# Output projections that start from their own operands' semaphores instead of a meeting of the engines, behind forgetting attention, HGRN, differential attention and spatial gating

## The reference, cut to what matters

```python
def fox_mixer(h, w_in, b_f, w_out):       # forgetting attention
    ...
    o = o.transpose(1, 0, 3, 2, 4).reshape(B, S, D)
    return o @ w_out
def hgrn2_mixer(h, w_in, lb, onorm_g, w_out):
    ...
    o = o * lax.rsqrt(jnp.mean(o * o, axis=-1, keepdims=True) + RMS_EPS)
    ...
    o = o.reshape(B, S, D).astype(h.dtype) * jax.nn.silu(g)
    return o @ w_out
# second block
    mix = jnp.concatenate([a_out, b_out], axis=-1) @ w_out_even[j]   # diff attention, gated conv
    ...
    mix = spatial_gating(h, w_in_odd[j], sgu_ln_g[j], sgu_ln_b[j], sgu_w[j],
                         sgu_b[j], w_out_odd[j])
```

## Time and profile before

| | |
|---|---|
| median of 3 runs | 3640.46 us (3634.68 to 3640.66) |
| profiled execution | 3639.07 us, its span 3637.3 us |
| PE busy | 3478.2 us (96%) |
| DVE busy | 1954.3 us (54%) |
| ACT busy | 1253.4 us (34%) |
| mean granted TensorE clock | 0.983 of full |

### The profile page before, as it was taken

One profiled execution on the slowest core, in us unless ns is written; L12 is line 12 of the kernel. 1 busy time (PEld: TensorE's weight loads), 2 busy tenths in 40 slices (PEclk: granted clock), 3 DMA queues, 4 the chain that ended last, 5 costly groups with the idle time before them and its releaser, 6 DMA issues.

```text
span 3637.3 us, 56212 instructions
## 1 busy us (share of the span) xinstructions
PE 3478.2 (96%) x23343; PEld 2871.5 (79%) x23343; DVE 1954.3 (54%) x2685; ACT 1253.4 (34%) x1598; POOL 0.2 (0%) x4
## 2 busy tenths in 40 slices
PE   9999999998999999999999989999999887999998
PEld 7778888887788877778887768887887875888887
DVE  4565736436574653565344355344676666845434
ACT  3474424324342441443223343223532113333222
POOL 0000000000000000000000000000000000000000
PEclk9999999999999999999999999999999999999999
DMA  4102232221123222113222212222233002022231
GB/s 155 58 1 93 93 103 93 93 98 42 58 93 104 93 95 98 41 58 104 93 99 98 81 58 93 93 96 101 91 108 137 4 5 91 5 81 93 93 104 70
DMA packets 50432, 297.10 MB, mean 82 GB/s; under 512 B 6848, under 2 KB 7872, under 8 KB 17349
## 3 DMA queue, kind: packets, MB, share of 16 engines
q1 hardware_dynamic: 39376, 269.92, 21.9%
q10 hardware_dynamic: 10868, 24.41, 1.8%
HBM read 283.99 MB, written 10.33 MB: 81 GB/s over the span
## 4 chain that ended last, share of the span: by engine, by line
PE 90%; DVE 7%; ACT 2%; issue 1%; DMA 0%; DVEq 0%; ACTq 0%; PEldq 0%
PE PS L334 13%; PE PS L336 13%; PE PS L335 13%; PE PS L449 8%; PE PS L450 7%; PE PS L451 7%; PE PS L1902 2%; PE PS L1903 2%; PE PS L1904 2%; PE PS L2409 1%; PE PS L1219 1%; PE PS L2826 1%; PE PS L2412 1%; PE PS L1199 1%; PE PS L215 1%
## 5 line engine op out<-in xcount | busy, mean ns | idle before, releaser
L171 DVE TENSOR_TENSOR WL<-W,WH 128x2048 fp32r<-128x2048 f32 x254 | 582.1, 2292 | 729.3 <-ACT WH L161 723.6
L161 ACT ACTIVATE WH<-W 128x2048 fp32r<-128x2048 f32 x254 | 485.8, 1912 | 1105.2 <-PE PS L451 578.0
L334 PE MATMUL PS<-XH,WH 128*128 128x512 f32 x2144 | 837.8, 391 | 4.3 <-issue 4.3
L335 PE MATMUL PS<-XL,WH 128*128 128x512 f32 x2144 | 835.1, 390 | 0.0
L336 PE MATMUL PS<-XH,WL 128*128 128x512 f32 x2144 | 835.0, 389 | 0.0
L334 PEld LDWEIGHTS PS<-XH,WH 128*128 128x128 f32 x2144 | 403.1, 188 | 93.7 <-issue 10.6
L335 PEld LDWEIGHTS PS<-XL,WH 128*128 128x128 f32 x2144 | 403.1, 188 | 84.5 <-issue 1.0
L336 PEld LDWEIGHTS PS<-XH,WL 128*128 128x128 f32 x2144 | 403.0, 188 | 84.0
L689 DVE TENSOR_TENSOR PS<-PS,R 128x512 f32<-128x512 f32 x248 | 170.9, 696 | 442.4 <-PE PS L336 439.8
L449 PE MATMUL PS<-HH,WH 128*128 128x512 f32 (+1 forms) x960 | 374.7, 390 | 1.2
L451 PE MATMUL PS<-HH,WL 128*128 128x512 f32 (+1 forms) x960 | 373.6, 389 | 0.0
(11 more groups left out here) (480 smaller groups left out, 4607.9 us busy)
## 6 DMA issues: line engine op xcount, KB each, us to landing
W<-in_weights SPq DMA_DIRECT2D x254, 1024.0 KB, 4.9
gate_spill<-slots ACTq DMA_DIRECT2D x16, 256.0 KB, 2.1
gates<-gate_spill ACTq DMA_DIRECT2D x2, 2048.0 KB
x_spill<-X ACTq DMA_DIRECT2D x1, 2048.0 KB, 8.0
X<-x_spill ACTq DMA_DIRECT2D x1, 2048.0 KB
out<-X ACTq DMA_DIRECT2D x8, 256.0 KB, 2.1
W<-in_weights SPq DMA_DIRECT2D x2, 512.0 KB, 5.0
X<-in_x ACTq DMA_DIRECT2D x4, 256.0 KB, 7.2
```

Of the source, the lines that this page charges most:

```text
L161: P.e.activation(K.WH[:, s, :], K.W[:, s, :], ACT.Copy).then_inc(P.sem("hi_ready"), P.adds("hi_ready"))
L171: P.e.tensor_tensor(K.WL[:, s, :], K.W[:, s, :], K.WH[:, s, :].bitcast(F32), ALU.subtract).then_inc(P.sem("weights_split"), P.adds("weight ...
L334: P.e.matmul(out, wh[:, k, c], xh[:, k, r], start=(k == 0), stop=False)
L335: P.e.matmul(out, wh[:, k, c], xl[:, k, r], start=False, stop=False)
```

## The change

PE no longer meets ACT and DVE between the four stages and their projections; it ends the stage with `stage_end_open`. ACT and DVE still meet, with PE's contribution, as before. In place of the meeting:

- The subtraction that writes a tile of `XL` now signals `tile_lo`, and PE waits for two of these before each panel (before each of the first two panels in `DiffOut`, where the attention gives four tiles).
- In the first panel, the banks that are still being read come last within each `kk`, and PE waits for their reader's signal just before the first matmul into each.

The same matmuls and the same elementwise work are done.

```diff
-def narrow_pe(K, P, nk, xh, xl, after_wide, late=None):
+def narrow_pe(K, P, nk, xh, xl, after_wide, late=None, tiles=0, held=()):
...
+        if first and held:
+            behind = [bank for bank, _, _ in held]
+            order = [(kk, t) for kk in range(2) for t in [t for t in range(8) if t not in behind] + behind]
+        if k0 < tiles:
+            P.e.wait_ge(P.sem("tile_lo"), P.due("tile_lo", 2))
...
+            for bank, name, k in held:
+                if first and kk == 0 and t == bank:
+                    P.e.wait_ge(P.sem(name), P.due(name, k))
...
 class ForgettingAttention(Stage):
+    tiles_given = 8
+    def banks_held(self):
+        return [(self.OUT[u], "head_taken", 1) for u in range(2)]
...
         def low_part(pair):
             P.e.wait_ge(P.sem("att_out_hi"), P.due("att_out_hi"))
-            P.e.tensor_tensor(K.XL[:, pair, 0:S], K.att_f[:, :], K.XH[:, pair, 0:S].bitcast(F32), ALU.subtract)
+            P.e.tensor_tensor(K.XL[:, pair, 0:S], K.att_f[:, :], K.XH[:, pair, 0:S].bitcast(F32), ALU.subtract).then_inc(P.sem("tile_lo"), P.adds("tile_lo"))
...
-        P.count("head_taken", 2)
...
 class Hgrn(Stage):
+    tiles_given = 8
+    def banks_held(self):
+        return [(1, "o_root", 8)]
...
 class DiffAttention(Stage):
+    tiles_given = 4
+    def banks_held(self):
+        return [(4, "mean_kept", 1), (7, "mean_kept", 1)]
...
-        P.count("mean_kept", 2)
...
 class SpatialGate(Stage):
+    tiles_given = 8
+    def banks_held(self):
+        return [(2, "sgu_biased", 1), (3, "sgu_biased", 1)]
...
+            if isinstance(st, (ForgettingAttention, Hgrn, DiffAttention, SpatialGate)):
+                after.tiles, after.held = st.tiles_given, st.banks_held()
...
-                if onto_wide or st.between_panels or after is not None and after.between_panels or isinstance(after, PostNorm) or isinstance(st, PostNorm) and isinstance(after, (Wide, MixerProjections, Epilogue)) or (isinstance(after, Narrow) and after.after_wide):
+                if onto_wide or st.between_panels or after is not None and after.between_panels or isinstance(after, PostNorm) or isinstance(st, PostNorm) and isinstance(after, (Wide, MixerProjections, Epilogue)) or (isinstance(after, Narrow) and (after.after_wide or after.tiles)):
                     P.stage_end_open()
```

More of the change, by code:

```diff
@@ L466, in body @@
         panel(4 * i + 4, False, False)
+    assert pairs == 1 or not tiles
     P.loop(pairs, body, weights_split=2, tile_done=4)
@@ L752 @@
     then = None
+    tiles, held = 0, ()
     gives_sums = property(lambda self: not self.before_post)
@@ L758, in pe @@
     def pe(self, K, P):
-        narrow_pe(K, P, self.nk, self.xh, self.xl, self.after_wide)
+        narrow_pe(K, P, self.nk, self.xh, self.xl, self.after_wide, None, self.tiles, self.held)
         if not self.before_post:
@@ L1326, in low_part @@
             P.e.wait_ge(P.sem("o_hi"), P.due("o_hi"))
-            P.e.tensor_tensor(K.XL[:, t, 0:S], K.f1[:, t, :], K.XH[:, t, 0:S].bitcast(F32), ALU.subtract)
+            P.e.tensor_tensor(K.XL[:, t, 0:S], K.f1[:, t, :], K.XH[:, t, 0:S].bitcast(F32), ALU.subtract).then_inc(P.sem("tile_lo"), P.adds("tile_lo"))
         for t in range(8):
@@ L1570, in low_part @@
             P.e.wait_ge(P.sem("o_hi"), P.due("o_hi"))
-            e.tensor_tensor(K.XL[:, h, 0:S], K.in2[:, h, :], K.XH[:, h, 0:S].bitcast(F32), ALU.subtract)
+            e.tensor_tensor(K.XL[:, h, 0:S], K.in2[:, h, :], K.XH[:, h, 0:S].bitcast(F32), ALU.subtract).then_inc(P.sem("tile_lo"), P.adds("tile_lo"))
         pad_rows(0)
@@ L1670, in pe @@
         narrow_pe(K, P, self.nk, self.xh, self.xl, self.after_wide,
-                  lambda: P.e.wait_ge(P.sem("conv_lo"), P.due("conv_lo")))
+                  lambda: P.e.wait_ge(P.sem("conv_lo"), P.due("conv_lo")), self.tiles, self.held)
     def act(self, K, P):
@@ L1761, in dve @@
                 P.e.wait_ge(P.sem("sgu_hi"), P.due("sgu_hi"))
-                P.e.tensor_tensor(K.XL[:, t - 2, 0:S], K.v2[:, t - 2, :], K.XH[:, t - 2, 0:S].bitcast(F32), ALU.subtract)
+                P.e.tensor_tensor(K.XL[:, t - 2, 0:S], K.v2[:, t - 2, :], K.XH[:, t - 2, 0:S].bitcast(F32), ALU.subtract).then_inc(P.sem("tile_lo"), P.adds("tile_lo"))
     def act(self, K, P):
```

## The result

The changed kernel takes 3618.32 us, the median of 5 runs (3616.3 to 3620.14), against 3640.46 before: the ratio is 0.9947 with a 95% interval of 0.9936 to 0.9958. The profiled execution took 3619.13 us, with a span of 3617.4, so that 19.9 of the 22.1 us are there to be read. Each later run was timed beside the kernel before on its own chip, and its ratio is to that.

What follows compares the result with a forecast made beforehand. The prediction took TensorE (90% of the chain) as the bound, costing idle time and low clock. Gaps of 14.6 and slow starts of 7.3 us, together 21.9, off 3639.07 gave 3617.2; it said 3618, range 3610 to 3629.

Steps and rivals of the forecast that it cites:

- the forecast's case: At the four projections, gaps and most slow starts go and no other wait comes: 21.9 us gained, chance 0.67.
- The gaps: PE's idle time at the meeting before the four projections, 15.04 us less 0.1 each: 14.6 us gained (13.0 to 15.0).
- The slow start: First panels behind the gaps run at 1.2 GHz; removing this gains 2.6, 1.0, 2.2 and 1.5, together 7.3 us (0 to 8.6).
- All behind the four stages: Everything behind the projections is released by PE's own progress and moves with it; no gain or loss counted.
- Held banks and tile waits: First panels' 17 added waits on tile_lo and banks, counted at nothing; 1.7 us if each cost 0.1.
- The owed splits and the convolution: Second panels' splits have 2.8 to 3.6 us slack, DiffOut's convolution 1.2: nothing counted, up to 2.3 us for the convolution.
- The low clock stays: Rival at the four projections: only the gap goes, the first panels stay at 1.2 GHz; 3624.5 to 3626 us, chance 0.15.
- the rule of the Trainium skill: Transposes don't count as clock activity, so the clock could fall in the stages' ends although PE doesn't stop.
- Moved, not removed: Rival at the second panels: PE waits for the owed splits instead; some 3637 to 3640 us, chance 0.07.
- The slow HGRN: Rival in HGRN: clock at 0.50 instead of 0.86 over 86 us loses 31 us; 3648 us, chance 0.04.

Runs made afterwards that it cites:

- e5: The changed kernel run again, unchanged: 3614.47 us.
- e9: Changed kernel with 5 matmuls that nothing reads ahead of the wait for the states in seven of HGRN's eight heads: 3610.69 us, ratio 0.9926.
- e10: Changed kernel with first-panel bank groups moved into the stages' last waits, except DiffAttention's, and unread matmuls in seven HGRN heads: 3601.73 us, ratio 0.9903.
- e6: The kernel before run again, unchanged: 3631.68 us.
- e1: Kernel before, meeting kept, with 13, 9, 14 and 13 unread matmuls filling PE's four gaps: 3624.78 us, ratio 0.997.
- e7: Changed kernel with the first product of DiffOut's convolution on DVE done twice (2.2 us more): 3625.15 us in a single execution.
- e2: Changed kernel with the first panel's banks in natural order 0 to 7, with the same waits: 3615.12 us, ratio 0.9945.
- e8: Kernel before with the first product of DiffOut's convolution on DVE done twice (2.2 us more): 3635.13 us in a single execution.
- e4: Changed kernel with some three-matmul bank groups of the first panel moved into the last waits of all four stages: 3607.64 us, ratio 0.992.
- e3_hgrn_only: Changed kernel with the stage end opened only behind HGRN; the other three projections meet as before: 3630.67 us, ratio 0.9984.

## Why the prediction was right

The time is the one predicted, 3618.32 against 3618, and the forecast's case is the one that happened: the waits of PE for the meeting are gone, and no other wait came.

- **The gaps** were put at 15.04 - 0.4 = 14.6 us. The cost that stays at each place is 0.26, 0.26, 0.29 and 0.26 us, not the 0.1 read off an input projection that goes into a `Narrow`, for 15.04 - 1.07 = 14.0. It was inside the bounds, and the nearest row was too cheap by a factor of 2.7; why a start costs 0.10 there and 0.26 here no run shows.
- **The slow start** was put at 7.3 us; the first panels show 2.45 + 0.10 + 2.06 + 1.40 = 6.0. At the three places with the full clock 5.9 us came, against 6.3. The term that was mis-sized is HGRN's, 0.1 instead of 1.0. I had let the slow stretch end a fixed 4.4 us after the mean's first matmul; it runs 6.8 us, from 924.40, and leaves 4.3 us in the projection instead of 2.5. How much it leaves is the execution's: in e5 it is 2.5 us (panel 12.20), the forecast's size. e9 and e10 show where it comes from: with the body filled but the end not, the panel is at 0.85, and with the end filled too the whole segment is at 1.00.
- **What made up for that**: HGRN's body was 1.27 us shorter (less 0.35 for the slower mean), and SpatialGate's segment lost 0.7 more than gap and clock. Together the places gave 14.0 + 6.0 + 0.9 + 0.7 = 21.6, beside a forecast of 21.9. Both extras go with the clock of the execution: SpatialGate's stage ahead of the gap takes 39.83 us at 0.96 in after and 40.54 at 0.92 in before, and e6 shows the body 3.5 and SpatialGate 1.4 us shorter in the unchanged kernel. That the sum met its forecast so closely is in part luck.
- **All behind the four stages** was put at 0 and is 1.9 us longer, the scan 2.5, with the same instructions; in e1 the scan took 245.47, in e5 248.26 and in e7 254.50, so the change isn't the cause.
- **Held banks and tile waits** were put at nothing, and cost nothing; e2 shows that not even the natural order waits.
- **The owed splits and the convolution** were put at nothing with slacks of 2.8 to 3.6 and 1.2 us. DiffOut's owed split ends at 1553.81 + 2.29 = 1556.1, with 3.05 us to the second panel at 1559.15; behind forgetting attention it ends at 272.26, with 3.5 to 275.72. The low part of the convolution ends at 1568.6, the third panel begins one panel of 10.88 us behind the second, at 1570.0: slack 1.4. e7 and e8 confirm it from outside, with 0.7 us of wait for 2.2 of delay in the changed kernel, and none in the one before.
- **The rivals.** "The low clock stays" held behind HGRN and nowhere else; e1 shows that the clock's cost goes at the three other places when PE is kept busy, even with the meeting in place. The light matmuls and transposes just ahead of those three starts didn't lower the clock (forgetting attention, a quarter of whose matmuls are transposes, has 1.00 over its whole segment), so the rule of the Trainium skill that the prediction weighed against itself ("TensorE: Matmul & The Clock Gate", Part 4) didn't decide here: the panels behind them show 1.00. "Moved, not removed" would have shown at the second panels, where nothing waits. The slow HGRN was a real mechanism with a price far too high: over the executions its body goes from 69.43 to 75.32 us, not to the 31 us more at which it was priced.

One thing stays open: why the same HGRN body gets a clock of 0.82 in one execution and 0.90 in another. The runs show only that the length goes with the clock, and that with the waits filled it was 67.87 us in both executions traced, e9 and e10.

## What to carry to other kernels

Let the matrix engine wait for the signals of its own operands instead of a meeting of all engines; the gap goes, and with it the half clock behind it, here 14.0 and 6.0 us for four gaps of 3.5 to 4.4. Before putting a price on the second part, read the clock of the work ahead of the gap: where that is already low, the rest of the slow stretch falls on what follows. Then go further: independent matmuls of the next stage, or even ones that nothing reads, placed in the stage's remaining waits, gave another 8 to 16 us here by the ratios (e9 8, e4 10, e10 16), and the reordering of banks gave nothing.

## What the hardware showed that I had not expected

- Extra matmuls made a stage faster. HGRN's body with 35 more took 67.87 us at 1.00, instead of 71.45 to 75.17 at 0.90 to 0.82 in the four executions shown of the two kernels as they are.
- Its length follows the granted clock, in all nine executions traced with the same stage code. At a clock c the share 2 x (1 - c) of a stretch is at 1.2 GHz, which gives:

| execution | body us | clock | at 1.2 GHz, us |
|---|---|---|---|
| e1_fill_gap | 69.43 | 0.92 | 11.1 |
| e6_before_again | 71.45 | 0.90 | 14.3 |
| e3_hgrn_only | 72.03 | 0.88 | 17.3 |
| e8_conv_late_before | 73.21 | 0.86 | 20.5 |
| e2_natural_order | 73.63 | 0.86 | 20.6 |
| after | 73.68 | 0.86 | 20.6 |
| before | 74.95 | 0.84 | 24.0 |
| e5_after_again | 75.17 | 0.82 | 27.1 |
| e7_conv_late_after | 75.32 | 0.82 | 27.1 |
| e9_hgrn_filled (35 matmuls more) | 67.87 | 1.00 | 0 |

- The low clock costs this body less than half its time there: between e1 and e5, 16.0 us more of it make the body 75.17 - 69.43 = 5.7 us longer, and against the filled e9 24.0 us cost before 7.1. In its waits PE has time to spare; in the panel behind it, where PE has none, 4.3 us of low clock cost 13.02 - 10.97 = 2.1.
- The scan, with the same 7968 matmuls, took 245.47 to 254.50 us over the executions named above, and the clock accounts for only a part: e1 and before both have 0.97 and lie 3.4 us apart. Most of the few us by which runs of one kernel differ can come from these two places.
